# One batch of value products per step in sliding-window attention (branch A)

## The reference

```python
# branch A: 8 query heads of 64, 2 key/value heads (each serves a group of 4 query heads)
logits = jnp.einsum('bcqkgd,bcskd->bckgqs', qc, kband) * SCALE      # a band of keys per chunk of queries
logits = logits + rel_bias_block(table, CHUNK, BAND, pad)
probs = sink_softmax(logits, sink)                                  # softmax with one more, learned, logit
out = jnp.einsum('bckgqs,bcskd->bcqkgd', probs, vband)              # weights times values
# merge: sigmoid(ga) * (oa @ w_br_a) + sigmoid(gb) * (ob @ w_br_b), then @ w_out
# ga, gb: further columns of the same input projection
```

## Time and profile before

| | |
|---|---|
| median of 3 runs | 1637.88 us (1636.92 to 1638.98) |
| profiled execution | 1639.09 us, of which span 1637.3 us |
| PE busy | 1583.7 us (97% of the span) |
| DVE, ACT, POOL busy | 713.8, 596.5, 384.0 us |
| mean granted PE clock | 0.991 |
| branch A's steps, first and second pass | about 78 to 148 us, 198 to 268 us of the span |

### The profile page before, as it was taken

The page is one execution under the profiler, slowest core; times in us unless marked ns, Lnnn a source line. Parts: engine busy times, 40 slices in busy tenths (PEclk is TensorE's granted clock), DMA queues, the critical chain, the costliest instruction groups (busy, mean ns, idle before and its releaser), DMA issues.

```text
span 1637.3 us, 26585 instructions
## 1 busy us (share of the span) xinstructions
PE 1583.7 (97%) x9822; PEld 1459.0 (89%) x9822; DVE 713.8 (44%) x1207; ACT 596.5 (36%) x1275; POOL 384.0 (23%) x263
## 2 busy tenths in 40 slices
PE   6998999999999999999999999999999999999996
PEld 5997988989898998997879899898998989899894
DVE  6364363564837467545541322313233231322318
ACT  6354354564746557334333121221211212121123
POOL 2101101102020110530014132232422324132334
PEclk9998999999999999999999999999999999999998
DMA  6112112112121222436222111110201111111124
GB/s 187 46 49 57 50 53 67 49 54 65 35 65 57 57 75 85 145 104 206 78 74 75 39 51 38 38 61 29 64 26 51 38 51 51 38 51 38 38 103 148
DMA packets 128889, 110.02 MB, mean 67 GB/s; under 512 B 14456, under 2 KB 117152, under 8 KB 128832
## 3 DMA queue, kind: packets, MB, share of 16 engines
q1 hardware_dynamic: 121920, 100.58, 19.9%
q10 hardware_dynamic: 6912, 8.65, 1.5%
HBM read 87.41 MB, written 21.80 MB: 67 GB/s over the span
## 4 chain that ended last, share of the span: by engine, by line
PE 83%; issue 8%; ACT 4%; DVE 3%; DMA 1%; POOL 0%; SPq 0%; ACTq 0%; DVEq 0%; POOLq 0%
PE m_ya L1553 20%; PE m_yb L1553 10%; PE m_yb L1575 9%; PE b_gm L954 9%; PE a_gm L454 6%; PE a_gm L490 5%; PE m_ya L1575 4%; PE b_gm L1008 4%; PE m_ya L1606 3%; PE m_yb L1606 3%; PE b_ob L1079 2%; PE b_tb L994 2%; PE a_ob L555 1%; ACT b_wgt L868 1%; PE b_zb L975 1%
## 5 line engine op out<-in xcount | busy, mean ns | idle before, releaser
L1373 POOL TENSOR_TENSOR w_lo<-f_raw,w_hi 128x1024 fp32r<-128x1024 f32 x66 | 157.9, 2399 | 406.0 <-ACT w_hi L1424 406.0
L1553 PE MATMUL m_ya<-x_hi,w_hi 128*128 128x352 f32 x704 | 227.3, 323 | 1.2 <-DVE x_lo L1688 0.9
L1553 PE MATMUL m_ya<-x_lo,w_hi 128*128 128x352 f32 x704 | 225.6, 320 | 0.0
L1553 PE MATMUL m_ya<-x_hi,w_lo 128*128 128x352 f32 x704 | 225.6, 320 | 0.0
L1424 ACT ACTIVATE w_hi<-f_raw 128x1024 fp32r<-128x1024 f32 x66 | 68.2, 1050 | 213.2 <-PE m_yb L1543 209.3
L1553 PEld LDWEIGHTS m_ya<-x_hi,w_hi 128*128 128x128 f32 x704 | 132.0, 188 | 2.5 <-issue 1.0
L1553 PEld LDWEIGHTS m_ya<-x_hi,w_lo 128*128 128x128 f32 x704 | 132.3, 188 | 0.4
L1553 PEld LDWEIGHTS m_ya<-x_lo,w_hi 128*128 128x128 f32 x704 | 132.0, 187 | 0.0
L1741 DVE TENSOR_TENSOR f_yacc<-m_yb,f_yacc 128x512 f32<-128x512 f32 x132 | 90.9, 690 | 82.0 <-PE m_yb L1575 81.6
L1553 PE MATMUL m_yb<-x_hi,w_hi 128*128 128x352 f32 x352 | 113.6, 323 | 0.0
L1553 PE MATMUL m_yb<-x_hi,w_lo 128*128 128x352 f32 x352 | 113.0, 321 | 0.0
(11 more groups left out here) (252 smaller groups left out, 3850.8 us busy)
## 6 DMA issues: line engine op xcount, KB each, us to landing
f_raw<-in_w_gate_up_dram SPq DMA_DIRECT2D x44, 512.0 KB, 3.9
w_raw<-in_w_in_dram SPq DMA_DIRECT2D x32, 512.0 KB, 3.9
f_raw<-in_w_down_dram SPq DMA_DIRECT2D x22, 512.0 KB, 3.3
m_gate<-gate_scratch SPq DMA_DIRECT2D x16, 528.0 KB, 4.4
gate_scratch<-a_gst ACTq DMA_DIRECT2D x24, 176.0 KB, 1.9
gate_scratch<-b_gst ACTq DMA_DIRECT2D x24, 176.0 KB, 1.9
xtok<-in_x_prompt_dram SPq DMA_DIRECT2D x8, 512.0 KB, 3.4
w_raw<-in_w_out_dram SPq DMA_DIRECT2D x8, 512.0 KB, 4.1
```

Source lines behind the costliest of these rows:

```text
L1373: pool.tensor_tensor(w_lo[:, j % 3, :, :].rearrange("p k n -> p (k n)"), raw[:, j % 2, :], w_hi[:, j % 3, :, :].rearrange("p k n -> p (k n ...
L1553: last = pe.matmul(gm[c][:, 0:CW], w[:, j % 3, k, :], x[:, k, chunk(c)], start=(k == 0 and n == 0), stop=(k == KT - 1 and n == 2))
```

## The change

Both pairs' value products of a step stand in one batch, in different columns of `ob`: the first pair's in columns 0 to 127, the second's in 128 to 255. The three gate products that stood between them stand in front, so nine follow the transposes. PE waits for `o_out` once in a step; for the weights (`wt_out`) it still waits once per pair. One copy takes both pairs out of `ob`. `o_done` and `o_out` move once in a step, 9 times (`NT`) in a pass, and whoever waits for them counts so.

```diff
@@ SyncE, ahead of the loads of the cached keys and values
-                    sp.wait_ge(o_done, past(g * NSTEP))
+                    sp.wait_ge(o_done, past(g * NT))
@@ ScalarE, a step: the copies of the weights, then the copy out
-                                act.wait_ge(o_done, past(g * NSTEP + max(s - 1, 0)))
+                                act.wait_ge(o_done, past(g * NT + (i - 1)))
...
-                            for t in range(2):
-                                s, q = 2 * (i - 1) + t, ROWS[i - 1]
-                                act.wait_ge(o_done, past(g * NSTEP + (s + 1)))
-                                act.activation(ot[:, bass.ds(g * 2 + t, 1), toks(i - 1)].rearrange("p o t -> p (o t)"),
-                                               ob[:, 0:q], ACT.Copy).then_inc(o_out, 1)
+                            act.wait_ge(o_done, past(g * NT + i))
+                            act.activation(ot[:, bass.ds(g * 2, 2), toks(i - 1)],
+                                           ob[:, 0:2 * P].rearrange("p (o t) -> p o t", t=P)[:, :, 0:ROWS[i - 1]],
+                                           ACT.Copy).then_inc(o_out, 1)
@@ TensorE, a step, after the transposes
-                        gates(g, first + FILL[0], FILL[1] + (FILL[2] if i == 0 else 0))
+                        gates(g, first + FILL[0], FILL[1] + FILL[2])
                         if i >= 1:
+                            pe.wait_ge(o_out, past(g * NT + (i - 1)))
                             for t in range(2):
                                 s, q = 2 * (i - 1) + t, ROWS[i - 1]
-                                if t:
-                                    gates(g, first + FILL[0] + FILL[1], FILL[2])
                                 pe.wait_ge(wt_out, past(g * NSTEP + (s + 1)))
-                                pe.wait_ge(o_out, past(g * NSTEP + s))
...
-                                        last = pe.matmul(ob[a * HD:(a + 1) * HD, 0:q], v,
+                                        last = pe.matmul(ob[a * HD:(a + 1) * HD, t * P:t * P + q], v,
...
-                                last.then_inc(o_done, 1)
+                            last.then_inc(o_done, 1)
@@ what branch B waits for
-        a_out = (o_out, past(KV_A * NSTEP))
+        a_out = (o_out, past(KV_A * NT))
```

## The result

| | before | after |
|---|---|---|
| median (runs) | 1638.98 us (5; 1636.92 to 1639.99) | 1629.97 us (5; 1627.14 to 1631.03) |
| profiled execution, span | 1639.09, 1637.3 us | 1630.52, 1628.7 us |

The ratio is 0.9946 with a 95% interval of 0.9935 to 0.9957: by that ratio 8.9 us less (7.0 to 10.7). The predicted 1631.3 is 1.3 us from the median after, and the sign is as forecast. That the time itself came so close is partly luck: the median before came out at 1638.98, 1.1 us above the 1637.88 from which the prediction counted. But the predicted gain of 6.5 lies just outside the interval, and rival B's 9.4 (1637.88 less 1628.5) inside it. So the first question of the traces is where 2 us more came from.

What follows compares the result with a forecast made beforehand. TensorE's own instruction line was taken to bound branch A's step loop; 5.4 us from the steps plus 1.1 from the last steps made 6.5, from 1637.88 to 1631.3 us (chance 0.70, own range 1629.5 to 1633.5; overall 1628.0 to 1634.6).

Steps and rivals of the forecast that it cites:

- rival B: At branch A's loop return, PE's instruction fetch may go ahead of SyncE's loads, 2.8 us less: 1628.5; chance 0.10.
- the seam: In branch A's steps, one batch of value products replaces two: 0.34 us saved per step, 16 steps, 5.4 us.
- Rival A: In the merged batch, the wait between halves drains PE; a step saves only 0.21 us: 1633.4; chance 0.09.
- C: Branch A's steps are paced through ScalarE and VectorE, so only the last steps' 1.1 us stay: 1636.8; chance 0.07.
- The cover: 0.5 us of slack before PE's second four transposes; the wider copy out of `ob` eats 0.10, so it holds.
- The stop: PE's 5.65 us idle after pass 1, read as its jump back to the loop top; taken as unchanged.
- the 0.54: At each pass's last step, the second batch no longer waits for the first's copy: 0.54 us, 1.1 over two passes.
- The clock behind the stop: After branch A's stops PE runs at the 0.50 clock for a while; this may fall otherwise by 1 or 2 us.
- D: Shifted code makes branch B's loop lose its top; its two returns cost 7.6 us each, 15.3 slower: 1646.6; chance 0.04.

Runs made afterwards that it cites:

- written out: PE's two passes of branch A unrolled in place of its loop: in the kernel after 1624.2 us (again 1624.26), in the kernel before 1631.8 us.
- the late return: Kernel after, with PE waiting for the last copy of the value products before turning back at a pass's end: 1632.59 us, ratio 0.9968.
- later loads: Kernel before, with SyncE waiting for the first pass's last value products before loading the second pass's weights: 1637.69 us, ratio 1.0001.

## Why the prediction was right, and where not

*What bounds the kernel; the seam.* Right. PE never waits in the steps, 16 seams of 0.34 to 0.36 us went, and moving the gate products, or splitting the copy, changes that gain or leaves it alone just as the sum says. Rival A fell with the 1.02 us batch, and C with the steps.

*The cover.* Right for full steps. It was not worked out for the last step of a pass, where PE has fewer products ahead of the transposes and they wait 0.21 us. A pass's sum is then 8 x 0.35 + 0.54 - 0.21 = 3.1; 3.2 was read.

*The stop.* This is the term that was mis-sized. The prediction let 5.65 us stand and "pass the 0.54 on"; it measured 3.58, with a second stop of 0.44 later. That it is a return and a fetch was right. That two packets lie in it was not: the second, in 153.6:153.8, goes after PE has restarted at 153.43. B was listed for the right reason, but with a chance of 0.10, since "nothing shows that the loads delayed it". In fact the one packet in the stop went 2.5 us after PE fell idle, in a stretch in which the loads flowed from 147.6; that delay was the evidence. So the forecast and B both came true: 6.5 and a further 2.1. B's price of 2.8, half the stop, rested on the second packet, and was 0.7 too high. (A slip besides: 1637.88 less 6.5 is 1631.4, not 1631.3.)

*The clock behind the stop.* The forecast had it only as spread. The stretch at 0.50 before, then after (columns as in the earlier trace rows):

```profile
148.00:158.00 10.00, 4.57 (x16) 4.60 (x17) 0.00 (x0) 3.93 (x5) 4.72 (x2) 0.50 0.55 133
```

```profile
147.30:150.60 3.30, 2.85 (x10) 2.88 (x11) 0.00 (x0) 1.06 (x1) 0.89 (x1) 0.50 0.86 196
```

Of PE's work 4.57 us fell into it before and 2.85 after; half of each is lost. The projections bear this out: 42.2 us written out at full clock, 44.61 before (2.4 more, of which 2.3 are half of 4.57) and 44.29 after (2.1 more: 1.4, half of 2.85, and 0.6 by the second stop, since 151.11 to 151.87 is 0.76 in place of 0.16).

*D, and the rest.* Branch B returned to its top without a stop, as before. After branch A the kernel after is 0.6 us longer; its profile shows a dip of the granted clock (0.50 to 0.73, at 850 to 853 us) where the kernel before has none. Nothing ties this to the change: the trace of the kernel before, written out, has a dip there too (852 to 857), that of the changed kernel with the late return has none, and the two traces of the kernel after, written out, differ by 1.5 us behind branch A.

## What to carry to other kernels

Where PE never waits, count how often its program goes over to small tiles and back, and gather their products in one visit: here a visit more to the 128x64 tiles is 0.35 to 0.38 us, and a further record in it 0.05. Other shapes need a price of their own. A loop return on PE can bring a transfer like any other: look for its packet in the instruction queue, and at what was issued just before it. For a loop of two passes, writing it out took away the stop and the slow clock behind it, here 5.5 us in the kernel before (1637.31 less 1631.8, on one chip).

## What was not expected of the hardware

- The return's price depends on tenths of a us. It stops PE for 3.0 to 3.8 us where PE falls idle 0.3 to 1.3 us before the first packets of the loads; for 5.65 where it falls idle 0.2 behind them, and for 6.55 where the copy that it waits for ends as they start.
- Branch A's return stops PE and branch B's doesn't. A pass of A has some 800 matmul records in the trace, one of B some 700; what distinguishes the two loops was not tried.
- The clock came back to full 2.9 us after PE's restart in the kernel after, 4.6 in the kernel before, and 5.2 in the one with later loads. One trace of each can't say why.
- Behind branch A the clock can fall for some us in one execution and not in the next of the same kernel (8 slices of 1 us against none); the trace with them is 1.5 us longer there.
